# Order of latent norms and modulation pieces, of weight requests, and of the reads of loop bounds, in a two-layer encoder kernel

## The chip, the cores and the metric

One core of a Trainium2 chip runs the kernel. The metric is the device time of one execution in microseconds (us). Engines are named as in the profile: PE is TensorE (PEld its weight loads), DVE is VectorE, ACT is ScalarE, POOL is GpSimd, and SP is SyncE, which here only issues DMAs. A queue name with q (SPq, ACTq) is the side of an engine that issues DMAs.

## The reference

A trunk of two layers over 256 tokens of width 1024, all in float32. Each layer's six modulation vectors, and two more for the key/value side, are `silu(c)` times a 1024-column block of a large matrix:

```
mod = silu(c) @ w_mod[layer] + b_mod[layer]          # 1024 x 6144 per layer; w_mod_kv: 1024 x 2048
# layer 0: h += g1 * retention(modulate(rms_norm(h)));  h += g2 * moe(modulate(rms_norm(h)))
# then once: keys and values
a    = modulate(rms_norm(h)) @ w_kv_a                # 128 latents and 64 rotary columns
c_kv = rms_norm(a[:, :128]); k_rope = rope(a[:, 128:])
k_nope, v = split(c_kv @ w_kv_b)                     # 8 heads
# layer 1: q from rms_norm(xn @ w_q_a) @ w_q_b, softmax attention under a block mask, @ w_o
h += g1 * mix;  h += g2 * moe(modulate(rms_norm(h)))
out = rms_norm(h) * final_norm
```

The mixture of experts takes the best of 4 groups and the best 2 of its 4 experts for each token. 16 experts have three matrices of 2 MB each, `w_gate`, `w_up` and `w_down`, so each layer reads some 100 MB of expert weights.

## The kernel before

**Ring and pieces.** All large weights stream through `ring`, six slots of 2 MB. SP issues the loads in one written order; ahead of each it waits (`released`) until the slot's last user is done. In the stretch that the diff touches the order is `MLA_ITEMS`: the four latent projections (kva, qa, kvb, qb), modulation pieces 20 to 25, the two halves of the output projection (wo0, wo1), pieces 26 and 27. A vector's product with `silu(c)` comes in two pieces; each has four steps on DVE (`mod_main`, a multiply at L1514 or multiply-adds at L1516) that sum into `part`. Vector 10 is pieces 20 and 21, vector 11 is 22 and 23, vector 12 is 24 and 25, vector 13 is 26 and 27. PE then sums the partitions of `part` with a product by ones: `gate_sum` (L604) for gates 10 and 13, whose result DVE adds to `gate` (`gate_store`, L1532), and `row_sum` (L611) for shift and scale, vectors 11 and 12. ACT copies the two row sums out and turns them with two small DMAs (`turned`, L1231); DVE uses them in `vectors` (L1538) and, after `turn_ffn` on PE (L635), prepares the router in `router_prep`.

**Key/value and query side.** PE forms kv latents (L1015), rotary keys (L1021) and query latents (L1029). DVE multiplies the rotary keys by sine and cosine, does all of piece 22, and only then the norms of the latents (L1806 to L1813), for which ACT has meanwhile summed the squares. PE turns the normed latents (L1039, L1044), forms the keys of 8 heads in four banks (L1053), the values (L1060), rotary queries (L1070) and queries (L1082); DVE and ACT copy the banks out, and POOL forms the rotary keys and queries. Before the first scores (L1094) stands row sum 11. After the eight heads PE runs the output projection (L1143) in eight blocks of four matmuls (`wo0`, then `wo1`, for two halves of the tokens and two of the columns); row sum 12, `turn_ffn` and `fixed_logits` (L787) stand between the blocks. A float32 matmul is two records in the trace.

**The experts.** SP loads pair 0's gates and ups (j = 0 to 3) into the ring, each when its slot is released. Pair 0's downs have room outside the ring, `down0` and `down1`; their load waits, in the second layer, for attention's end (`att_o`). Then follow pair 1's gates and the rest. After routing, `rounds(pair, ...)` runs PE's loop over slots of 64 tokens: gather (L865), gates (L890), ups (L903), downs (L921). Its bounds are numbers in memory, which DVE writes at L1714 (`bounds_ready`) and each engine reads into a register (`value_load`). The second layer's counts go on from the first's, so the first bound of `bounds[1]` equals entry `PAIRS` of `bounds[0]`. Each slot of the ring is released by semaphores that PE raises in `rounds`. `keep_warm` is a matmul whose result nobody uses.

Of the kernel before, what the change touches and what calls it, by code (L numbers as in the profile page):

```python
# [19 lines left out]
RH, RDK = 4, 256  # L20
MH, NOPE, ROPE, VH = 8, 128, 64, 128
# [4 lines left out]
PAIRS = NE // 2  # L26
SLOTS = 64
ROUNDS = SEQ // SLOTS
# [61 lines left out]
MOD_STORED = {}  # L90
# [39 lines left out]
def build_kernel(nc, t, out):  # L130
    with ExitStack() as ctx:
# [228 lines left out]
        def _(sp):  # L360
# [79 lines left out]
            for l in range(2):  # L440
                base = MOE_AT[l]

                for j in range(4):
                    released(base - RING + j)
                    load(base + j, matrix(l, 0, j))
                if l == 0:
                    sp.wait_ge(o_done, 2 * RH)
                else:
                    sp.wait_ge(att_o, MH)
                sp.dma_start(down0.rearrange("p (a k) n -> p a k n", a=2), matrix(l, 0, 4)).then_inc(spare_in[0], 16)  # L450
                last = matrix(l, 0, 5)
                sp.dma_start(down1[0], last[:, 0]).then_inc(spare_in[1], 16)
                for j in range(2):
# [86 lines left out]
        def _(pe):  # L540
# [5 lines left out]
            def keep_warm(n, b):  # L546

                for _ in range(n):
                    pe.matmul(bank[b][:], ones, cst[:, 0:512], start=True, stop=True)  # L549
# [241 lines left out]
            def experts(l):  # L791
                n = 1 + 2 * l

                def turn_h(tt, f):

# [50 lines left out]
                pe.matmul(bank[4][:, NE:2 * NE], ones, chosen[:, 0, :], start=False, stop=True).then_inc(ranked, 1)  # L846
                keep_warm(1, 5)
                pe.wait_ge(y_ready, 2 * n + 2)
                pe.wait_ge(bounds_ready, l + 1)
                pe.wait_ge(table_ready, l + 1)  # L850
                if l:
                    pe.wait_ge(mod_stored, MOD_STORED[(13, 1)])
                if l == 0:
                    pe.sem_inc(S["info_done"], 1)

                def rounds(pair, begin, end, here, w, last=False):
# [3 lines left out]
                    with pe.Fori(begin, end) as u:  # L860
# [56 lines left out]
                        def down(n2, f):  # L917
# [7 lines left out]
                            return ins  # L925

                        up(0, range(KT)).then_inc(S["up_done"], 1)
                        up(1, range(KT // 2))
# [56 lines left out]

                rounds(0, bound(slice(0, 1), 0) if l else 0, bound(slice(1, 2), 1), here0, w0)
                rounds(1, bound(slice(1, 2), 1), bound(slice(2, 3), 1),
# [132 lines left out]
            pe.wait_ge(qr_mult, 4)  # L1120
            row_sum(11, mla_bank[6])
            pe.wait_ge(qb_act, 2)
# [15 lines left out]
            for i in range(2):  # L1138
                w = item(f"wo{i}", 0).rearrange("p (k n) -> p k n", k=4)
                for tt in range(TT):  # L1140
                    for n in range(2):
# [6 lines left out]
                        elif tt == 1 and n == 1:  # L1148
                            ins.then_inc(wo_used, 1)
                        if (i, tt, n) == (0, 1, 0):  # L1150
                            row_sum(12, mla_bank[6])
# [250 lines left out]
        def _(dve):  # L1402
# [396 lines left out]
            for i in range(2):  # L1799
                w = trig[:, 1, i:i + 1, :].to_broadcast([P, 2, SEQ])  # L1800
                dve.tensor_tensor(mprod[:, i, :].rearrange("p (f s) -> p f s", f=2),
                                  mla_bank[5][:].rearrange("p (f s) -> p f s", f=2), w, ALU.mult).then_inc(kr_mult, 1)
            mod_main(22)

# [13 lines left out]
            gate_store(10, 1, mla_bank[3])  # L1818
            for b in (2, 4):
                dve.wait_ge(kv_done, b)  # L1820
                dve.tensor_copy(knT[:, 2 * (b - 1):2 * b, :], mla_bank[b][:].rearrange("p (k s) -> p k s", k=2)).then_inc(kv_dve, 1)
            for b in (1, 3):
                dve.wait_ge(kv_done, 4 + b + 1)
                dve.tensor_copy(vm[:, b // 2, 512:1024], mla_bank[(5, 6, 7, 0)[b]][:]).then_inc(kv_dve, 1)
            mod_main(23, (0, 1))

            dve.wait_ge(kr_ready, 5)
            for f in range(2):
                dve.wait_ge(qb_done, 1 + f)
                for i in range(2):  # L1830
                    w = trig[:, 1, i:i + 1, :].to_broadcast([P, 2, SEQ])
                    dve.tensor_tensor(mprod[:, 2 * f + i, :].rearrange("p (f s) -> p f s", f=2),
                                      mla_bank[5 + f][:].rearrange("p (f s) -> p f s", f=2), w, ALU.mult).then_inc(qr_mult, 1)
            mod_main(23, (2, 3))
            for b in (2, 4):
# [27 lines left out]
            for hd in range(MH):  # L1863
                head_scale(hd)
                if hd + 2 < MH:
                    head_max(hd + 2)
            for m in range(24, N_MOD):
                mod_main(m)
# [201 lines left out]
```

## Time and profile before

| | us |
|---|---|
| median of 3 runs (lowest, highest) | 928.96 (927.59, 932.24) |
| the profiled execution | 930.08 |
| its span, first to last instruction | 928.3 |
| PE busy | 859.1 (93%) |
| DVE, ACT, POOL busy | 325.8, 172.5, 162.2 |
| share of the chain that ended last: PE, DMA, DVE, issue | 76%, 16%, 3%, 2% |
| mean granted clock of PE | 0.967 |

The stages of the span, by the timeline: first layer's retention to about 285, its routing to 296, its experts to 537; the key/value and query side from there to 597; attention to 623; output projection to 654; second routing to 669; second experts to 919; final norm to the end. DMA has 317.15 MB to move; in the expert stages it runs at some 420 GB/s over long stretches.

### The profile page before, as it was taken

The page shows a single profiled execution, that of the slowest core. Times are in us where ns is not written, and L with a number is a line of the kernel's source. Part 1 is how long each engine was busy: PE and PEld are TensorE (multiplying, and loading weights), DVE is VectorE, ACT ScalarE, POOL GpSimd, SP SyncE. Part 2 cuts the span into 40 slices and gives each one's busy share as a digit, 9 for nine tenths or more (in the row PEclk, how much of TensorE's full clock was granted, in tenths as well). Part 3 has the DMA queues.
Part 4 walks back from the last instruction along what each step waited for, and adds up shares of the span by engine and source line. Part 5 has one row for each costly group of instructions (what it writes and reads, how often), then busy time and mean ns, then how long its engine had stood idle before and what let it go on. Part 6 is the DMA issues. An engine that isn't in the chain of part 4 may idle for free.

```text
span 928.3 us, 12079 instructions
## 1 busy us (share of the span) xinstructions
PE 859.1 (93%) x4367; PEld 480.4 (52%) x4368; DVE 325.8 (35%) x592; ACT 172.5 (19%) x342; POOL 162.2 (17%) x272
## 2 busy tenths in 40 slices
PE   6999999999998999999888876999699999999985
PEld 4787444444445455544454365774455554555442
DVE  2836676864104111111111185677411111111103
ACT  2100121222003222212011030250322212211111
POOL 0023000000016322221011041301622221111011
PEclk9999999999998999999899877999899999999999
DMA  9999989989383799999999954596799999399995
GB/s 323 387 357 376 373 330 376 348 316 383 146 320 139 307 424 402 420 422 422 423 423 415 331 207 182 187 361 267 309 397 423 416 396 423 141 390 423 423 379 179
DMA packets 69686, 317.15 MB, mean 342 GB/s; under 512 B 9976, under 2 KB 10107, under 8 KB 44303
## 3 DMA queue, kind: packets, MB, share of 16 engines
q1 hardware_dynamic: 61274, 304.42, 82.0%
q0 software_dynamic: 4976, 8.40, 3.6%
q10 hardware_dynamic: 3396, 3.80, 1.3%
q8 instruction: 26, 0.43, 0.2%
q14 instruction: 14, 0.11, 0.0%
HBM read 311.31 MB, written 15.20 MB: 352 GB/s over the span
## 4 chain that ended last, share of the span: by engine, by line
PE 76%; DMA 16%; DVE 3%; issue 2%; ACT 1%; SPq 1%; ACTq 0%; DVEq 0%; POOL 0%; POOLq 0%
PE bank L903 13%; PE bank L722 12%; DMA ring<-in_moe_w_up 11%; PE bank L921 8%; PE bank L890 8%; PE bank L763 6%; PE bank L865 5%; PE bank L663 4%; DMA h<-outs 3%; PE bank L1143 3%; PE bank L715 1%; PE bank L1096 1%; PE bank L913 1%; DMA outs<-arena,row_id 1%; PE bank L549 1%
## 5 line engine op out<-in xcount | busy, mean ns | idle before, releaser
L903 PE MATMUL bank<-ring,arena 128*64 128x256 f32 x1088 | 130.1, 394 | 16.7 <-DMA ring<-in_moe_w_up 16.7
L921 PE MATMUL bank<-ring,arena 128*64 128x512 f32 x480 | 112.2, 609 | 5.8 <-issue 5.8
L1763 DVE TENSOR_TENSOR arena<-bank,arena 128x256 f32<-128x256 f32 x34 | 20.9, 614 | 272.4 <-PE bank L903 272.4
L903 PEld LDWEIGHTS bank<-ring,arena 128*64 128x64 f32 x1088 | 83.2, 142 | 64.2 <-issue 34.1
L1516 DVE SCALAR_TENSOR_TENSOR part<-ring,cpad,part 128x1024 f32<-128x1024 f32 x84 | 111.2, 1324 | 3.2 <-DVE part L1516 0.7
L722 PE MATMUL bank<-ring,xnT 128*128 128x512 f32 x256 | 111.2, 593 | 0.0
L890 PE MATMUL bank<-ring,arena 128*64 128x512 f32 x480 | 106.3, 596 | 0.0
L722 PEld LDWEIGHTS bank<-ring,xnT 128*128 128x128 f32 x256 | 48.5, 190 | 59.3 <-issue 59.2
L865 PEld LDWEIGHTS bank<-arena,y 128*128 128x128 f32 x544 | 66.5, 203 | 19.6 <-issue 19.6
L865 PE MATMUL bank<-arena,y 128*128 128x128 f32 x544 | 69.7, 290 | 5.1 <-issue 5.1
L921 PEld LDWEIGHTS bank<-ring,arena 128*64 128x64 f32 x480 | 34.0, 140 | 64.3 <-issue 62.3
L890 PEld LDWEIGHTS bank<-ring,arena 128*64 128x64 f32 x480 | 33.2, 137 | 60.2 <-issue 59.9
L1313 ACT ACTIVATE arena<-bank,modc,scale 128x128 f32<-128x128 f32 x68 | 25.6, 456 | 186.9 <-PE bank L865 186.9
L1929 POOL DMA_INDIRECT outs<-arena,row_id x17 | 18.0, 1056 | 220.7 <-DVE arena L1773 138.9
L1773 DVE SCALAR_TENSOR_TENSOR arena<-bank,info,gate 128x512 f32<-128x512 f32 x34 | 25.5, 751 | 78.7 <-PE bank L921 78.7
L1905 POOL TENSOR_TENSOR h<-h,acc 128x512 f32<-128x512 f32 x6 | 7.6, 1264 | 242.6 <-DVE acc L1642 242.6
L1924 POOL TENSOR_SCALAR arena<-slot_id,place_two 128x64 f32<-128x64 f32 x108 | 45.8, 445 | 5.5 <-POOL slot_id L1939 3.0
L663 PE MATMUL bank<-xnT,ring 128*128 128x256 f32 x192 | 41.9, 380 | 0.0
L663 PEld LDWEIGHTS bank<-xnT,ring 128*128 128x128 f32 x192 | 36.5, 190 | 5.3 <-DVE xnT L1469 0.4
L1754 DVE TENSOR_SCALAR arena<-bank,scale,modc 128x128 f32<-128x128 f32 x68 | 23.3, 404 | 28.9 <-PE bank L865 28.9
L1143 PE MATMUL bank<-ring,arena 128*128 128x512 f32 x64 | 28.5, 598 | 0.5 <-issue 0.5
L763 PE MATMUL bank<-ring,y 128*128 128x512 f32 x64 | 28.0, 592 | 0.0
(304 smaller groups left out, 871.4 us busy)
## 6 DMA issues: line engine op xcount, KB each, us to landing
ring<-in_moe_w_up SPq DMA_DIRECT2D x64, 1024.0 KB, 12.1
ring<-in_moe_w_gate SPq DMA_DIRECT2D x56, 1024.0 KB, 14.8
ring<-in_moe_w_down SPq DMA_DIRECT2D x56, 1024.0 KB, 15.7
ring<-in_w_mod SPq DMA_DIRECT2D x48, 1024.0 KB, 11.9
ring<-in_ret_w_in SPq DMA_DIRECT2D x24, 1024.0 KB, 7.8
ring<-in_w_mod_kv SPq DMA_DIRECT2D x8, 1024.0 KB, 12.7
ring<-in_ret_w_out SPq DMA_DIRECT2D x8, 1024.0 KB, 12.9
arena<-in_moe_w_down SPq DMA_DIRECT2D x2, 2048.0 KB, 12.1
```

What stands on the lines that cost most here:

```text
L663: ins = pe.matmul(o[:, f * SEQ:(f + 1) * SEQ], w[:, k, c:c + P], xnT[:, k, :], start=(f == 0 and k == 0), stop=(f == 1 and k == KT - 1))
L722: ins = pe.matmul(pair[tt][:], xnT[:, k, tok(tt)], w[:, k, :], start=(k == 0), stop=(k == KT - 1))
L763: ins = pe.matmul(bank[2 * tt + n][:], yT(4 * i + kk)[:, tok(tt)], w[:, kk, n * 512:(n + 1) * 512], start=(i == 0 and kk == 0), stop=(i == ...
L865: ins = pe.matmul(bank[4 + k // 4][:, (k % 4) * P:(k % 4 + 1) * P], y[:, tt, k * P:(k + 1) * P], chosen_slots[:, tt, :], start=(tt == 0), ...
L890: ins = pe.matmul(bank[0][e * 64:(e + 1) * 64, :], xgT[:, k, e * 64:(e + 1) * 64], w(e, k), start=(k == 0), stop=(k == KT - 1))
L903: ins = pe.matmul(bank[1 + f][e * 64:(e + 1) * 64, 0:256], xgT[:, k, e * 64:(e + 1) * 64], w(2 + e, k)[:, f * 256:(f + 1) * 256], start=(k ...
L921: ins = pe.matmul(bank[6 + n2][e * 64:(e + 1) * 64, :], hidT[:, k, e * 64:(e + 1) * 64], w(4 + e, k)[:, n2 * 512:(n2 + 1) * 512], start=(k ...
L1143: ins = pe.matmul(mla_bank[(5, 7, 0, 4)[2 * tt + n]][:], oT[:, 4 * i + kk, tok(tt)], w[:, kk, n * 512:(n + 1) * 512], start=(i == 0 and kk ...
L1313: ins = A(xgT[:, k, :], bank[5][:, tok(j)], ACT.Identity, bias=modc[:, MOD_COL[l] + 24 + k:MOD_COL[l] + 25 + k], scale=scale[:, 1 + 2 * l, ...
L1516: ins = dve.scalar_tensor_tensor(o, w[:, k, :], c, o, ALU.mult, ALU.add)
L1773: dve.scalar_tensor_tensor(yg[:, s], bank[6 + n2][:], info[:, 1:2], gate[:, 2 * l + 1, s], ALU.mult, ALU.mult).then_inc(S["yg_ready"], 1)
L1924: ins = pool.tensor_scalar(dst[:, tt, e * SLOTS:(e + 1) * SLOTS], slots, places[:, tt, e:e + 1], None, ALU.is_equal)
```

## The change

Five edits, in the order of the file:

1. SP: in the second layer the two loads of pair 0's down weights, with their wait for attention's end, go ahead of the four loads of pair 0's gates and ups. In the first layer the order stays.
2. PE, `experts`: the first bound of the second layer is read at the start of the stage, from the first layer's array. The second bound is read right after the wait for `bounds_ready`, ahead of the waits for `y_ready` and `table_ready`. The second layer has one more `keep_warm` matmul.
3. PE: the second layer's wait for gate 13's stores moves from ahead of `rounds` to ahead of the up matmuls in each round.
4. PE: row sum 11 moves from ahead of the first scores to after the output projection's first block; row sum 12 moves one block later.
5. DVE: piece 22 no longer stands ahead of the latent norms. Its first two steps stand ahead of the two key copies, its last two where the first two of piece 23 stood; those move to where the last two of 23 stood, and these to after the last head.

```diff
--- before.py
+++ after.py
@@ -440,16 +440,26 @@
             for l in range(2):
                 base = MOE_AT[l]
 
-                for j in range(4):
+                def ahead(j):
                     released(base - RING + j)
                     load(base + j, matrix(l, 0, j))
+
+                last = matrix(l, 0, 5)
+
+                def outside_down():
+                    if l == 0:
+                        sp.wait_ge(o_done, 2 * RH)
+                    else:
+                        sp.wait_ge(att_o, MH)
+                    sp.dma_start(down0.rearrange("p (a k) n -> p a k n", a=2), matrix(l, 0, 4)).then_inc(spare_in[0], 16)
+                    sp.dma_start(down1[0], last[:, 0]).then_inc(spare_in[1], 16)
+
+                if l:
+                    outside_down()
+                for j in range(4):
+                    ahead(j)
                 if l == 0:
-                    sp.wait_ge(o_done, 2 * RH)
-                else:
-                    sp.wait_ge(att_o, MH)
-                sp.dma_start(down0.rearrange("p (a k) n -> p a k n", a=2), matrix(l, 0, 4)).then_inc(spare_in[0], 16)
-                last = matrix(l, 0, 5)
-                sp.dma_start(down1[0], last[:, 0]).then_inc(spare_in[1], 16)
+                    outside_down()
                 for j in range(2):
                     released(base - 2 + j)
                     load(base + 4 + j, matrix(l, 1, j))
@@ -791,6 +801,8 @@
             def experts(l):
                 n = 1 + 2 * l
 
+                begin0 = pe.value_load(bounds[0][0:1, PAIRS:PAIRS + 1], min_val=PAIRS, max_val=ROUNDS * PAIRS) if l else 0
+
                 def turn_h(tt, f):
 
                     for j in range(4):
@@ -844,12 +856,11 @@
                 ins.then_inc(counted, 1)
                 pe.matmul(bank[4][:, 0:TT * NE], tri, chosen[:].rearrange("p t e -> p (t e)"), start=True, stop=False)
                 pe.matmul(bank[4][:, NE:2 * NE], ones, chosen[:, 0, :], start=False, stop=True).then_inc(ranked, 1)
-                keep_warm(1, 5)
+                keep_warm(1 + l, 5)
+                pe.wait_ge(bounds_ready, l + 1)
+                second = pe.value_load(bounds[l][0:1, 1:2], min_val=1, max_val=ROUNDS * PAIRS * (l + 1))
                 pe.wait_ge(y_ready, 2 * n + 2)
-                pe.wait_ge(bounds_ready, l + 1)
                 pe.wait_ge(table_ready, l + 1)
-                if l:
-                    pe.wait_ge(mod_stored, MOD_STORED[(13, 1)])
                 if l == 0:
                     pe.sem_inc(S["info_done"], 1)
 
@@ -924,6 +935,8 @@
                                                     start=(k == 0), stop=(k == 3))
                             return ins
 
+                        if l:
+                            pe.wait_ge(mod_stored, MOD_STORED[(13, 1)])
                         up(0, range(KT)).then_inc(S["up_done"], 1)
                         up(1, range(KT // 2))
                         turn_hidden(0)
@@ -983,7 +996,7 @@
                 def bound(at, least):
                     return pe.value_load(bounds[l][0:1, at], min_val=least, max_val=ROUNDS * PAIRS * (l + 1))
 
-                rounds(0, bound(slice(0, 1), 0) if l else 0, bound(slice(1, 2), 1), here0, w0)
+                rounds(0, begin0, second, here0, w0)
                 rounds(1, bound(slice(1, 2), 1), bound(slice(2, 3), 1),
                        lambda j, f: arrived(base + 4 + j, halves=(f,)), lambda j, k: in_ring(base + 4 + j, j, k))
                 rounds(2, bound(slice(2, 3), 1), bound(slice(3, 4), 1), here2, w2)
@@ -1118,7 +1131,6 @@
                 pe.matmul(b[:, P:SEQ], v[:, 1, :], probT[:, hd % 2, SEQ:SEQ + P], start=False, stop=True).then_inc(att_o, 1)
 
             pe.wait_ge(qr_mult, 4)
-            row_sum(11, mla_bank[6])
             pe.wait_ge(qb_act, 2)
             pe.wait_ge(qb_dve, 2)
             pe.wait_ge(qr_ready, 2)
@@ -1147,7 +1159,9 @@
                             ins.then_inc(mix_done, 1)
                         elif tt == 1 and n == 1:
                             ins.then_inc(wo_used, 1)
-                        if (i, tt, n) == (0, 1, 0):
+                        if (i, tt, n) == (0, 0, 0):
+                            row_sum(11, mla_bank[6])
+                        if (i, tt, n) == (0, 1, 1):
                             row_sum(12, mla_bank[6])
                         if (i, tt, n) == (1, 0, 0):
                             turn_ffn(3, mla_bank[2])
@@ -1800,7 +1814,6 @@
                 w = trig[:, 1, i:i + 1, :].to_broadcast([P, 2, SEQ])
                 dve.tensor_tensor(mprod[:, i, :].rearrange("p (f s) -> p f s", f=2),
                                   mla_bank[5][:].rearrange("p (f s) -> p f s", f=2), w, ALU.mult).then_inc(kr_mult, 1)
-            mod_main(22)
 
             dve.wait_ge(lat_sq, 4)
             dve.tensor_scalar(var[:, 0:2], msq[:, 0:2], 1.0 / KVL, EPS, ALU.mult, ALU.add).then_inc(lat_ms, 1)
@@ -1817,12 +1830,13 @@
             gate_store(10, 0, mla_bank[5])
             gate_store(10, 1, mla_bank[3])
             for b in (2, 4):
+                mod_main(22, (b // 2 - 1,))
                 dve.wait_ge(kv_done, b)
                 dve.tensor_copy(knT[:, 2 * (b - 1):2 * b, :], mla_bank[b][:].rearrange("p (k s) -> p k s", k=2)).then_inc(kv_dve, 1)
             for b in (1, 3):
                 dve.wait_ge(kv_done, 4 + b + 1)
                 dve.tensor_copy(vm[:, b // 2, 512:1024], mla_bank[(5, 6, 7, 0)[b]][:]).then_inc(kv_dve, 1)
-            mod_main(23, (0, 1))
+            mod_main(22, (2, 3))
 
             dve.wait_ge(kr_ready, 5)
             for f in range(2):
@@ -1831,7 +1845,7 @@
                     w = trig[:, 1, i:i + 1, :].to_broadcast([P, 2, SEQ])
                     dve.tensor_tensor(mprod[:, 2 * f + i, :].rearrange("p (f s) -> p f s", f=2),
                                       mla_bank[5 + f][:].rearrange("p (f s) -> p f s", f=2), w, ALU.mult).then_inc(qr_mult, 1)
-            mod_main(23, (2, 3))
+            mod_main(23, (0, 1))
             for b in (2, 4):
                 dve.wait_ge(qb_done, 2 + b)
                 dve.tensor_copy(qnT[:, 2 * (b - 1):2 * b, :], mla_bank[b][:].rearrange("p (k s) -> p k s", k=2)).then_inc(qb_dve, 1)
@@ -1864,6 +1878,7 @@
                 head_scale(hd)
                 if hd + 2 < MH:
                     head_max(hd + 2)
+            mod_main(23, (2, 3))
             for m in range(24, N_MOD):
                 mod_main(m)
             vectors(3, cols[:, :, 10:12])
```

## Rows read from the trace of the kernel before

**Rows 1.** The timeline, key/value part; start us, us, engine, line, operation [idle before]
```profile
550.95 7.07 PE L1021 MATMUL bank<-arena,ring 128*128 128x256 f32 x32
...
565.60 0.20 ACT L1351 ACTIVATION_READ_ACCUMULATOR xnT<-bank 128x1 f32 x1
...
567.31 0.75 DVE L1514 TENSOR_SCALAR part<-ring,cpad 128x1024 f32<-128x1024 f32 x1 [7.71 <-issue]
...
568.09 3.92 DVE L1516 SCALAR_TENSOR_TENSOR part<-ring,cpad,part 128x1024 f32<-128x1024 f32 x3
...
572.18 0.17 DVE L1806 TENSOR_SCALAR stat<-stat 128x2 f32<-128x2 f32 x1 [0.16 <-DVE part L1516]
...
573.57 0.69 PE L1039 MATMUL bank<-cst,arena 128*128 128x128 f32 x2 [6.92 <-DVE arena L1811]
...
575.26 5.87 PE L1053 MATMUL bank<-arena,ring 128*128 128x256 f32 x16
...
576.29 1.28 DVE L1532 TENSOR_TENSOR gate<-bank,gate 128x512 f32<-128x512 f32 x2
...
585.55 3.71 PE L1070 MATMUL bank<-arena,ring 128*128 128x256 f32 x16 [0.99 <-DVE arena L1824]
```

**Rows 2.** Busy time by stretch; clock, DMA share and GB/s at the end
```profile
core 0: us, PE busy (x) PEld busy (x) DVE busy (x) ACT busy (x) POOL busy (x), PEclk, DMA share, GB/s
576.00:580.00 4.00, 4.00 (x11) 3.12 (x11) 2.27 (x4) 0.60 (x1) 3.84 (x5) 0.52 0.01 2
...
648.00:652.00 4.00, 4.00 (x12) 1.87 (x11) 0.69 (x1) 2.63 (x4) 1.78 (x2) 1.00 0.00 0
...
668.00:672.00 4.00, 2.54 (x12) 2.57 (x13) 0.00 (x0) 0.00 (x0) 2.07 (x2) 0.50 1.01 420
...
740.00:744.00 4.00, 4.00 (x32) 1.90 (x28) 0.61 (x1) 1.67 (x2) 0.00 (x0) 1.00 0.86 332
```

**Rows 3.** The timeline, end of the second routing
```profile
663.51 1.10 PE L549 MATMUL bank<-cst 128*128 128x512 f32 x2
...
664.31 0.16 DVE L1714 CAST bounds<-boundf 1x16 int32<-1x16 f32 x1
...
666.40 1.29 DVE L1532 TENSOR_TENSOR gate<-bank,gate 128x512 f32<-128x512 f32 x2 [0.21 <-issue]
...
669.47 6.64 PE L865 MATMUL bank<-arena,y 128*128 128x128 f32 x32 [4.85 <-issue]
```

**Rows 4.** The timeline, then the chain of waits, first routing
```profile
294.45 0.16 DVE L1714 CAST bounds<-boundf 1x16 int32<-1x16 f32 x1
...
296.48 5.45 PE bank L865 x32
```

**Rows 5.** Waits, from 540 us: total us, times, longest
```profile
PE bank L903 <- DMA ring<-in_moe_w_up: 5.7, 2, 4.6
```

**Rows 6.** The timeline, VectorE and GpSimd side by side
```profile
547.89 5.04 DVE L1516 SCALAR_TENSOR_TENSOR part<-ring,cpad,part 128x1024 f32<-128x1024 f32 x3
...
548.71 3.15 POOL L2032 COPY ring<-ring 128x512 f32<-128x512 f32 x2
```

**Rows 7.** The timeline, from the first scores to the output projection's end
```profile
596.12 1.05 PE L611 MATMUL bank<-part,cst 128*32 128x512 f32 x4
...
620.42 0.75 DVE L1514 TENSOR_SCALAR part<-ring,cpad 128x1024 f32<-128x1024 f32 x1
...
623.14 10.54 PE L1143 MATMUL bank<-ring,arena 128*128 128x512 f32 x24 [0.52 <-issue]
...
640.63 0.18 DVE L1538 TENSOR_TENSOR modc<-turned,cols 128x16 f32<-128x16 f32 x1
...
650.50 0.29 PE L787 MATMUL bank<-shifted,cst 128*128 128x16 f32 x2
```

**Rows 8.** The timeline, the small DMAs of the first layer
```profile
250.26 1.18 ACTq L1231 DMA_DIRECT2D turned<-arena  x2
...
256.71 0.19 DVE L1538 TENSOR_TENSOR modc<-turned,cols 128x16 f32<-128x16 f32 x1 [21.91 <-DMA turned<-arena]
```

**Rows 9.** DMA issues, from 540 us: KB each, median us to landing
```profile
acc<-in_moe_w_down SPq DMA_DIRECT2D x1, 1024.0 KB, 24.9
```

## Prediction

> **What bounds the kernel now.** I read the page's chain of work first: TensorE carries three quarters of it, and most of the remainder is waiting for expert weights. So a microsecond counts only where TensorE stands still, or where TensorE sets when a ring slot comes free. Then I read the order of instructions in the stretches that the diff touches.
>
> *Latents* [rows 1]. ScalarE ends the last sum of squares at 565.60 + 0.20 = 565.80. VectorE starts the norm step (L1806) only at 572.18: it has first taken up modulation piece 22, waited for its weights until 567.31, and spent 0.75 + 3.92 us on it. TensorE sits idle 6.92 us ahead of its latent transposes (L1039). It then runs the key matmuls (L1053) at the low clock: 16 records take 5.87 us, where 32 of the same tile size took 7.07 us at full clock (L1021). The clock row for 576 to 580 shows 0.52, nearly all of it the lower level, 1.2 of 2.4 GHz [rows 2].
>
> *Second routing* [rows 3]. The bounds are written at 664.31 + 0.16 = 664.47, and the first gather (L865) starts at 669.47, 5.0 us later. TensorE waits for VectorE's two gate adds (L1532, to 667.69) and reads two bounds after that. The gather then takes 6.64 us at clock 0.50 [rows 2]. In the first routing no gate add stands between: bounds at 294.61, gather at 296.48 (1.87 us later), 5.45 us long [rows 4].
>
> *Expert stage.* In the second one TensorE waits for up weights 5.7 us over two places [rows 5]. But the DMA queue is empty at 648 to 652, and has gaps again at 740 to 744 [rows 2]: there the stream has caught up with the slots that TensorE releases, so what follows is timed from TensorE.
>
> **The change part by part.** All terms are against the profiled execution (span 928.3, time 930.08), which lies 1.1 above the median of the runs.
>
> A. *Norms ahead of piece 22.* The norm step can start 0.17 us after the squares (it started about that long after VectorE's own last step): 565.97 instead of 572.18, **6.2 us**. TensorE's transposes come to 567.4. It is free by then: its idle time before L1039 began at 573.57 - 6.92 = 566.65. Bounds: 5.5 if handing over from ScalarE costs more, 6.4 if it costs nothing.
>
> B. *Clock of the key matmuls.* With 0.7 us of idle time in place of 6.92 I expect the clock to stay up. L1053 would take 7.07 / 2 = 3.5 instead of 5.9: 2.3 us less. Its third bank also waits for the gate add of vector 10 (L1532). That add shifts to about 570.1 to 571.4, where the first two banks end at 570.8, so 0.6 comes back. Gain **1.8** with the transposes' own; bounds 0 (clock falls anyway) and 2.6.
>
> C. *What takes piece 22's place.* Its first two quarters now stand ahead of the two key copies, its last two where 23's first half was, that half where 23's second was, and 23's second half behind the last head. The first quarter costs 0.75, the second 3.92 / 3 = 1.3. In the new frame VectorE does 571.4 to 572.2, copy, 572.9 to 574.2, copy; the value matmuls end at about 576.5, so both quarters and the value copies fit beside them. The query matmuls (L1070, 585.55 before) start near 577.5, 8.0 earlier (A + B). Cost taken: 0; bounds 0 and 0.7. One row speaks against it: a multiply-add piece took 5.04 us for three beside GpSimd's copies, against 3.92 without [rows 6], 0.37 more each, and GpSimd now forms the rotary keys beside these two quarters. That is 0.7 us, inside the cover that I count.
> The Trainium skill (SBUF — State Buffer, Who interferes with whom) says that a VectorE instruction with two SBUF inputs contends with a GpSimd one that reads SBUF, and that the loser blocks for the whole instruction. The trace agrees with the slowing; a block through several rotary steps would be worse than the 0.7 used here, and no row shows one.
>
> D. *Row sum 11* leaves the place before the first scores, where it ran 596.12 to 597.17 beside the last query copy, and joins the output projection, where TensorE has no gap: 24 records run on from 623.14 [rows 7]. Gain ahead 0 (at most 0.2), cost behind **1.0**. Row sum 12 comes one block (3.5 us) later. The first projection block ends at about 618.6 in the new frame, and VectorE has finished piece 23 by 620.42 - 8.0 + 2.6 (two steps of 1.3) = 615.0, so neither sum waits.
>
> E. *VectorE after attention* has 2.6 us more. Piece 27 ended by 640.63 and now ends near 635.2. The vectors then need row sum 12 (done 631.2) and the two small DMAs that follow it. In the first layer these went out at 250.26 and were used at 256.71, 6.45 us later [rows 8]; so 632.0 + 6.45 = 638.5, and router preparation, some 2 us, ends near 640.6. TensorE asks for it (L787, 650.50 before) at 643.5. Cost 0, cover 2.9 us; if the DMAs need more, the excess is lost.
> The Trainium skill (DMA: Bandwidth & Descriptors, Queues, rings and completion order) says that a DMA engine takes the queue rows in turn, packet by packet. By that rule the small DMAs don't wait behind SyncE's megabytes, and the first layer's 6.45 us agree.
>
> F. *SyncE.* Three megabytes of the first pair's down weights now go out when attention ends, into time in which the queue was later empty. Ahead of it SyncE waits for piece 23, since piece 27 reuses its slot: piece 27 is requested near 615.1 instead of ahead of attention's end, and is needed at 630. Gates 0 and 1 come after pieces 24 and 25. Some 9.4 MB at about 420 GB/s are in by 637.7, up 0 by 642.7, before the projection ends (647). So the expert stage starts with 7.4 us less DMA work behind it, while TensorE comes closer by G and H, 4.3 us. The stream still catches up before the fourth pair's gates, so the two stalls of 5.7 us stay, timed from TensorE. Cost and gain 0. Bounds: minus 1.2 (the small stall goes) and plus 4.3 (a rival).
>
> G. *Bounds ahead of the last waits.* The start of the second expert stage (the end of the first) is read long before, beside matmuls already queued. The wait for the gate store moves to the first up matmuls, some 10 us after the gather starts. One more warming matmul (1.10 us) ends at 665.6 in the old frame, and the read of the bound runs beside it. I take the first routing's 1.87 us from bounds to gather: gain 5.0 - 1.9 = **3.1**. Bounds: 2.1, if the read starts only when the warming is over (665.6, and the 1.77 us from 667.70 to 669.47 as its price), and 3.6. The wait stands in every round: cheap and beside queued matmuls, 0. The first routing's own gain: 0, bounds 0 and 0.3, since its warming matmuls already cover the read.
>
> H. *Clock of the first gather.* With a shorter idle stretch and one more matmul it is the likeliest to look like the first layer's: 6.64 - 5.45 = **1.2**. Bounds 0 and 3.3 (all of it at full clock).
>
> Sum: 6.2 + 1.8 - 1.0 + 3.1 + 1.2 = 11.3. Profiled 918.8; from the median 928.96 it gives **917.7 us**.
>
> **The rivals.**
> - *Both clocks stay low.* For: the first routing had fallen to half although idle for little, and the four transposes are thin work. Against: the clock is full at 648 to 652 and through the projection. Then A - D + G = 8.3: 920.7.
> - *Both clocks stay full.* B and H at their ends: 11.3 + 0.5 + 2.1 = 13.9: 915.0.
> - *The expert stage is paced by transfers.* What TensorE wins after attention's end (G + H, 4.3) returns as longer waits for up weights. For: 5.7 us of such waits now. Against: the gaps at 740 to 744, and F. 922.0.
> - *The norms were not what held the latents* (the change doesn't do there what it says: the next stage waits for something as late, such as GpSimd's keys). Then only G + H - D = 3.3: 925.7. Against: the idle times in [rows 1] name VectorE alone.
> - *Slower: piece 27 lands late.* It is the one large load pushed from before attention's end to after it, with 3 MB of down weights and the gates crowding in. The longest landing of this stage is 24.9 us [rows 9]. VectorE could start piece 27 as late as 636.5 without making L787 wait (643.5, less 2.0 for the vectors, less 5.2 for four steps), which is 21 us after the request. At 24.9 the loss is 3.5; the gain is used up from 21 + 11.3 = 33 us; at 40 us the kernel stands at 936. The bytes queued bound it at about 643, 28 us, so this is remote.
>
> **How the numbers follow.** Forecast 0.55; clocks low 0.15; clocks full 0.10; paced by transfers 0.12; norms not the cause 0.05; slower 0.03. The forecast's own range is 916 to 920. 8 in 10 takes in the full clocks below and the two partial cases above with a microsecond of scatter: 913.8 to 923.3. What a measurement can tell here is about 0.5%, 4.6 us: faster means under 924.3. All cases but the last two lie there: faster 0.92, same 0.05, slower 0.03.
>
> **What would show it.** A: L1806 within 0.3 us of ScalarE's last square, TensorE's idle time before L1039 under 1 us. B: L1053 in about 4 us, clock 1.0. C: L1070 starting 7.5 to 8.5 earlier. D: L1143 ends 7 earlier, not 8. E: no idle time ahead of L787. F: the empty stretch before the projection's end shorter, piece 27's step on VectorE without a wait, the two waits of the expert stage as long as now. G: 1.9 us from the bounds to the first gather; H: that gather at 5 to 6 us. It is wrong if the gather starts less than 8 us earlier than 669.47, or if the waits for up weights grow by more than 2 us.

## The result and the profile after

The changed kernel takes 922.89 us (median of 20 runs, 920.37 to 929.68), the kernel before 928.78 on the same chip (20 runs). The ratio is 0.9947, with a 95% interval of 0.9932 to 0.9963. It is faster, by 5.9 us; the forecast was 11.3. The range held the time at its upper edge. The profiled execution took 925.25 with a span of 923.5, so the two traces differ by 4.8.

The timeline of the changed kernel from the latents to the first gather (columns as in [rows 1]; line numbers are 10 to 15 higher than before, DVE L1552 for instance is L1538 of before, and shift again by a few in each experiment's kernel):

```profile
567.15 0.20 ACT L1365 ACTIVATION_READ_ACCUMULATOR xnT<-bank 128x1 f32 x1
567.39 0.17 DVE L1819 TENSOR_SCALAR stat<-stat 128x2 f32<-128x2 f32 x1 [6.19 <-ACT xnT L1365]
568.77 0.44 PE L1052 MATMUL bank<-cst,arena 128*128 128x128 f32 x2 [0.58 <-DVE arena L1824]
570.05 1.89 PE L1066 MATMUL bank<-arena,ring 128*128 128x256 f32 x8
...
572.24 1.26 DVE L1528 TENSOR_SCALAR part<-ring,cpad 128x1024 f32<-128x1024 f32 x1
572.38 1.99 PE L1066 MATMUL bank<-arena,ring 128*128 128x256 f32 x8 [0.44 <-DVE gate L1546]
574.14 1.81 DVE L1530 SCALAR_TENSOR_TENSOR part<-ring,cpad,part 128x1024 f32<-128x1024 f32 x1
...
578.78 3.70 PE L1083 MATMUL bank<-arena,ring 128*128 128x256 f32 x16 [0.98 <-DVE arena L1838]
...
616.36 3.67 PE L1155 MATMUL bank<-ring,arena 128*128 128x512 f32 x8 [0.52 <-issue]
...
617.20 1.63 SPq L454 DMA_DIRECT2D arena<-in_moe_w_down  x1
618.88 0.47 SPq L455 DMA_DIRECT2D arena<-in_moe_w_down  x1
...
633.16 1.58 ACTq L1245 DMA_DIRECT2D turned<-row_late  x2
...
646.76 0.18 DVE L1552 TENSOR_TENSOR modc<-turned,cols 128x16 f32<-128x16 f32 x1 [10.33 <-DMA turned<-row_late]
...
648.81 0.40 PE L797 MATMUL bank<-shifted,cst 128*128 128x16 f32 x2 [3.75 <-DVE shifted L1569]
649.06 5.38 PE L1155 MATMUL bank<-ring,arena 128*128 128x512 f32 x8
...
657.05 0.63 PE L813 MATMUL bank<-cst,h 128*128 128x128 f32 x4 [0.68 <-DVE h L1667]
...
665.83 0.16 DVE L1728 CAST bounds<-boundf 1x16 int32<-1x16 f32 x1
667.13 3.81 PE L876 MATMUL bank<-arena,y 128*128 128x128 f32 x32
```

Read against [rows 1], [rows 3] and [rows 7]: the norms, the bounds and the gather are as wanted or better. But VectorE now stands 10.33 us for the two small `turned` DMAs (the turned halves of the last vector), and TensorE 3.75 us behind it. The chain of waits of the changed kernel (start, us, what) passes through that transfer:

```profile
631.51 1.01 PE bank L621 x4
...
633.16 1.03 ACTq L1245
634.23 12.51 DMA turned<-row_late
...
648.76 0.61 DVE acc L1656
649.43 2.50 POOL h L1920 x2
651.95 1.15 ACT y L1304 x2
```

Busy time by stretch, columns as in [rows 2]:

```profile
638.00:642.00 4.00, 4.00 (x10) 1.85 (x11) 0.00 (x0) 0.00 (x0) 0.00 (x0) 1.00 1.02 424
...
644.00:646.00 2.00, 1.06 (x3) 0.19 (x1) 0.00 (x0) 0.00 (x0) 0.00 (x0) 1.00 0.70 276
646.00:648.00 2.00, 0.00 (x0) 0.00 (x0) 1.10 (x5) 0.00 (x0) 0.00 (x0) 1.00 0.03 5
648.00:652.00 4.00, 3.19 (x6) 1.49 (x7) 2.48 (x6) 0.05 (x1) 2.57 (x3) 0.70 0.00 0
668.00:672.00 4.00, 4.00 (x35) 3.54 (x35) 2.27 (x6) 1.73 (x4) 2.19 (x5) 1.00 1.01 422
```

The DMA share is full until 645.2 and falls to nothing by 646.7: SyncE's megabytes had all landed, and VectorE went on with the small DMAs' data at 646.76. Below, the backlog is what SyncE has requested and has not yet moved, and its end is the moment at which the DMA share has fallen to about half, here 645.4. The waits, answering to [rows 5] (total us, times, longest):

```profile
PE bank L914 <- DMA ring<-in_moe_w_up: 5.2, 2, 4.5
```

Where the 4.8 us came from, by TensorE's marks in both traces:

| stretch | before | after | gain | forecast |
|---|---|---|---|---|
| start to the last transposes before the key/value part (no edit in it) | 540.61 | 542.18 | -1.57 | 0 |
| to the output projection (A, B, C) | 82.53 | 74.18 | 8.35 | 8.0 |
| projection to its last turns, L801, now L813 (D, E) | 32.80 | 40.69 | -7.89 | -1.0 |
| to the gather (G) | 13.53 | 10.08 | 3.45 | 3.1 |
| the gather, to the first gate matmul (H) | 6.97 | 4.16 | 2.81 | 1.2 |
| the rest (F) | 251.86 | 252.21 | -0.35 | 0 |

### The profile page after: what moved, and what is told of

It reads as the page before. It is cut to its first block, busy times and chain, and to the rows that moved or that the text cites. A ratio compares the mean times of both kernels' runs of the same rounds, so it can differ in the third digit from the quotient of the medians.

```text
span 923.5 us, 12083 instructions
## 1 busy us (share of the span) xinstructions
PE 857.3 (93%) x4369; PEld 476.6 (52%) x4370; DVE 326.9 (35%) x592; ACT 172.5 (19%) x342; POOL 164.4 (18%) x272
## 4 chain that ended last, share of the span: by engine, by line
PE 74%; DMA 18%; DVE 3%; issue 2%; ACT 2%; SPq 1%; ACTq 0%; POOL 0%; DVEq 0%; POOLq 0%
PE bank L914 12%; PE bank L732 12%; DMA ring<-in_moe_w_up 8%; PE bank L932 8%; PE bank L901 8%; PE bank L773 6%; DMA h<-outs 6%; PE bank L876 5%; PE bank L673 4%; DMA outs<-arena,row_id 2%; PE bank L1155 2%; PE bank L725 1%; DMA turned<-row_late 1%; PE bank L559 1%; PE bank L1109 1%
## 5 line engine op out<-in xcount | busy, mean ns | idle before, releaser
L876 PEld LDWEIGHTS bank<-arena,y 128*128 128x128 f32 x544 | 64.0, 197 | 14.6 <-issue 14.6
L876 PE MATMUL bank<-arena,y 128*128 128x128 f32 x544 | 67.2, 283 | 0.1
L1920 POOL TENSOR_TENSOR h<-h,acc 128x512 f32<-128x512 f32 x6 | 7.5, 1264 | 249.4 <-DVE acc L1656 249.4
L1155 PE MATMUL bank<-ring,arena 128*128 128x512 f32 x64 | 30.4, 629 | 0.5 <-issue 0.5
```

The costliest lines, as they stand in the source:

```text
L876: ins = pe.matmul(bank[4 + k // 4][:, (k % 4) * P:(k % 4 + 1) * P], y[:, tt, k * P:(k + 1) * P], chosen_slots[:, tt, :], start=(tt == 0), ...
L1155: ins = pe.matmul(mla_bank[(5, 7, 0, 4)[2 * tt + n]][:], oT[:, 4 * i + kk, tok(tt)], w[:, kk, n * 512:(n + 1) * 512], start=(i == 0 and kk ...
```

## The experiments

Theory: three megabytes of down weights ahead of the gates lengthen SyncE's backlog, and the small DMAs that ScalarE issues land only when it is empty. Rival one: VectorE's later row sum 12 (edit D) makes `turned` late. Rival two: what G and H win is taken back by the expert stage. In the tables and texts, "after start" counts from the first matmul of the output projection.

**e1: the order of SyncE's loads as before.**

```
-                if l:
-                    outside_down()
                 for j in range(4):
                     ahead(j)
-                if l == 0:
-                    outside_down()
+                outside_down()
```

> The changed kernel with SyncE's order of before: pair 0's down weights behind its gates and ups. Theory (backlog): the two small DMAs that turn row sums 11 and 12 took 13.6 us from issue to use because some 10 MB, the 3 MB of down weights among them, had been requested ahead of them; without the downs they are used within about 6 us of their issue, VectorE's wait of 10.3 us shrinks to under 4, TensorE no longer waits ahead of the fixed logits (3.75 us now), its clock stays full, and the kernel takes 6 to 7 us less than the changed one, about 916. Rival (the downs' lead is needed): the expert stage loses up to 7.4 us (3 MB at 420 GB/s), so 920 to 924. Rival (late row sum): the wait stays at 8 us or more, 922 to 923.

Measured: 920.3 us (6 runs), ratio 0.9928 (0.9904 to 0.9953). Its timeline, then its waits for up weights:

```profile
631.74 1.58 ACTq L1242 DMA_DIRECT2D turned<-row_late  x2
...
639.17 0.19 DVE L1549 TENSOR_TENSOR modc<-turned,cols 128x16 f32<-128x16 f32 x1 [4.17 <-DMA turned<-row_late]
...
643.47 0.29 PE L794 MATMUL bank<-shifted,cst 128*128 128x16 f32 x2
```
```profile
PE bank L911 <- DMA ring<-in_moe_w_up: 7.8, 2, 4.5
```

From issue to use 7.4 us instead of 13.6, and TensorE's wait is gone. The same row sums stand in it, so rival one can't be the cause. But the waits for up weights grow from 5.2 to 7.8. In e4 below, where TensorE is as far along as in e1 (34.67 and 34.55 us from the projection's start to its last turns) and the downs are early, they are 5.2 again. So the early downs do help the expert stage, by 2.6 us in this pair of traces (the kernels that have the bounds' edit and all downs early show 4.9 to 6.2), which I had put at nothing.

**e2: the downs after the small DMAs have landed, ahead of the ups.**

```
                 for j in range(4):
+                    if l and j == 2:
+                        sp.wait_ge(vecs_in, 128)
+                        outside_down()
                     ahead(j)
```

> The changed kernel, but pair 0's downs (and then its ups) are requested only once the small DMAs have landed, behind the two gates. Backlog theory: small DMAs used 4 to 7 us after issue, no wait of TensorE at the fixed logits, 915.5 to 917, and the 3 MB still move ahead of the projection's end. If the downs' lead is worth something this one is faster than the kernel with the downs last, otherwise equal. Late row sum theory: 922 to 923, as the changed kernel.

Measured: 916.16 us (6 runs), ratio 0.989 (0.9864 to 0.9916), an interval apart from the changed kernel's. Its timeline, and its busy time by stretch:

```profile
629.41 1.58 ACTq L1246 DMA_DIRECT2D turned<-row_late  x2
...
632.47 0.38 SPq L454 DMA_DIRECT2D arena<-in_moe_w_down  x1
632.61 0.18 DVE L1553 TENSOR_TENSOR modc<-turned,cols 128x16 f32<-128x16 f32 x1
```
```profile
626.00:628.00 2.00, 2.00 (x7) 0.60 (x7) 1.77 (x2) 0.00 (x0) 0.00 (x0) 1.00 0.98 414
630.00:632.00 2.00, 2.00 (x6) 0.76 (x4) 1.93 (x3) 0.00 (x0) 0.00 (x0) 1.00 0.19 61
```

The small DMAs go out as the backlog ends, are in 3.1 us later (SyncE passes its wait at 632.47), and VectorE takes them up at 632.61, straight after piece 27. This gives both: no stall at the projection, and 5.4 us of waits for ups, about the changed kernel's.

**e3: row sum 12 one block earlier, as before the change** (`(i, tt, n) == (0, 1, 0)`).

> The changed kernel with row sum 12 one block (3.5 us) earlier, where it stood before; the small DMAs are issued 3.5 us earlier, behind the same megabytes. Backlog theory: they are used at the same moment as in the changed kernel, near 646 in its frame, when the queue has drained, so VectorE's wait grows and the time stays within 1 us of the changed kernel (922 to 923.5). Late row sum theory (fixed latency): they are used 3.5 us earlier and the kernel takes about 3.5 us less, 919.4.

Measured: 924.65 us (9 runs), ratio 0.9947 (0.9924 to 0.997).

```profile
631.31 1.58 ACTq L1245 DMA_DIRECT2D turned<-row_late  x2
...
648.10 0.18 DVE L1552 TENSOR_TENSOR modc<-turned,cols 128x16 f32<-128x16 f32 x1 [10.08 <-DMA turned<-row_late]
```

Issued 3.4 us earlier after start (13.37 against 16.80), used at the same time after start (30.16 against 30.40). The latency stretched from 13.6 to 16.8 us. So it is not a duration of the DMA but a wait for a point in time, the end of the backlog. Rival one is out.

**e4: the same turning by GpSimd's queue** (four DMAs of 64 partitions with a semaphore of their own, in place of ScalarE's two).

```
+                    pool.dma_start(turned[64 * a:64 * a + 64, 3, r, :],
+                                   row_late[...]).then_inc(vecs_late, 16)
```

> The changed kernel, but GpSimd issues the turning of row sums 11 and 12 (four small software DMAs) in place of ScalarE. If the backlog holds every queue's transfers, the vectors come near 646 again or later and the time stays at 922 to 925. If each queue gets its turn and only ScalarE's queue is held up by SyncE's, they land some 4 to 6 us after issue, near 638, and the time is 916 to 917.

Measured: 918.07 us (6 runs), ratio 0.9897 (0.9877 to 0.9918). Timeline and stretches:

```profile
630.77 2.19 POOL L2069 DMA_DIRECT2D turned<-row_late  x4 [44.64 <-ACT row_late L1241]
...
637.99 0.19 DVE L1555 TENSOR_TENSOR modc<-turned,cols 128x16 f32<-128x16 f32 x1 [4.22 <-DMA turned<-row_late]
```
```profile
636.00:638.00 2.00, 2.00 (x6) 0.82 (x5) 0.01 (x1) 0.00 (x0) 0.00 (x0) 1.00 1.03 411
640.00:642.00 2.00, 2.00 (x6) 0.95 (x5) 1.19 (x2) 0.00 (x0) 1.32 (x2) 1.00 1.01 422
```

The engines were saturated until about 643, with the early downs in front as in the changed kernel, and yet `turned` was there at 637.99, 7.2 us after the issue. The same bytes through another queue are not held. So full DMA engines as such are not the cause; what holds them is tied to ScalarE's queue under SyncE's backlog. The edit also makes four DMAs of 2 KB out of two of 4 KB, and no run keeps that apart from the change of queue.

The DMA packets in the traces show how they are held. A packet is one piece of a transfer on one of the 16 DMA engines; the counts are those of each queue.

| stretch | SyncE's packets | the small DMAs' packets |
|---|---|---|
| changed kernel, 633 (issue) to 637 | 226 | 0 |
| 637 to 645 | 454 | 55 |
| 645 to 647 | 36 | 205 |
| e4, 630.5 (issue) to 634 | 196 | 0 |
| 634 to 638 | 223 | 128 |

In both kernels the first small packet moves some 4 us after the issue. From then on ScalarE's queue does move, but with one packet for eight of SyncE's, 6 to 8 in a microsecond; the same rate stands in e3 (635 to 647) and e9 (634 to 637). So some 200 of its 260 packets are left at the backlog's end and then go within two microseconds. GpSimd's queue moves one packet for one of SyncE's at the best (101 against 111 in 635 to 637), and it has 128 in all.

**e9 and e11: two sizes between.** e9 puts 1 MB of the downs ahead (`down1`) and 2 MB (`down0`) behind the ups. e11 keeps all the downs ahead and makes the ups wait (`vecs_in`, 128).

> The changed kernel with only 1 MB of the downs ahead of the gates and ups, the other 2 MB behind them. Backlog theory (the small DMAs are used when the queue of megabytes has drained): 2 MB less is 5 us less, so the vectors come about 25 us after the output projection's start in place of 30.4, TensorE no longer waits ahead of the fixed logits, 917 to 919. Rival (a saturated DMA holds small transfers for some 13 us whatever is queued): 30 us after the start, 922 to 923.

> The changed kernel with the downs first, but the two ups requested only once the small DMAs have landed. Backlog theory: the 2 MB of up 0, requested at the same time as the small DMAs, no longer count; vectors about 25 us after the projection's start, 917 to 919. If only what was requested well before the small DMAs holds them, no change: 30 us, 922 to 923.

Measured: e9 919.8 us (4 runs), 0.9898 (0.9863 to 0.9932); e11 919.24 (4 runs), 0.9901 (0.9867 to 0.9935). Their small DMAs took 8.4 and 8.5 us, and were used 1.1 and 1.2 us after the backlog's end (near 637.6 and 636.7). Each has 2 MB less in front than the changed kernel, which is 5.0 us at 420 GB/s, and they are used 5.2 and 5.1 us earlier after start. All kernels with the new latent order and both row sums in the projection, in us after start (e8 is told below):

| kernel | issued | used | projection start to last turns |
|---|---|---|---|
| e2 | 16.80 | 20.00 | 33.97 |
| e8 | 16.80 | 20.97 | 33.97 |
| e1 | 16.81 | 24.24 | 34.55 |
| e4 | 17.07 | 24.29 | 34.67 |
| e7 | 16.80 | 24.36 | 34.65 |
| e9 | 16.80 | 25.22 | 35.51 |
| e11 | 16.80 | 25.32 | 35.61 |
| e3 | 13.37 | 30.16 | 40.44 |
| changed kernel | 16.80 | 30.40 | 40.69 |

In e2 and e8 the small DMAs find the backlog gone and take 3.2 and 4.2 us. The constants are read off this table: all nine lie on 33.97 + (used - 23.66), where that is positive, within 0.1 us. So the delay of `turned` passes one to one into the time from 23.66 on, and the changed kernel lost 6.7 us by it. It also shows how thin the cover is. In e9 and e11 the fixed logits (L797 of the changed kernel) have no wait; TensorE waits at the turns behind them. The chain after shows why: behind `turned` VectorE also holds the first gated sums of the projection (L1656), behind them stand GpSimd's additions (L1920) and ScalarE's square sum (L1304), and these come late first.

**e5, e6 and e7: the parts alone, each on the kernel before.** e5 has the early downs only; e6 the read-ahead of the bounds with the second warming matmul and the moved wait; e7 the latent norms, the pieces and the row sums.

> The kernel before with the first of the five edits alone: pair 0's downs requested when attention ends. Backlog theory: the queue then drains near 646 in the frame of before, the small DMAs issued at 635.3 are used near 646 in place of 640.6; router preparation ends near 648, ahead of the fixed logits at 650.5, so TensorE hardly waits (0 to 1 us) and the 3 MB of lead buy nothing or the small stall at 788: 927 to 929.5 (before: 928). If the early downs were a gain of their own: 924 or less.

> The kernel before with the bounds read ahead, one more warming matmul and the gate wait moved, nothing else. In the changed kernel the stretch from the last h transposes to the gather's end shrank from 20.5 to 14.2 us. If that is this edit's alone: 6.3 us less, 921.7. If the experts then come closer to their transfers (stalls for up weights 7.8 us instead of 5.2 where the downs go out late): 922 to 925, with the waits for up weights at 8 us or more. Forecast's terms G + H: 923.7.

> The kernel before with the order of norms, pieces and row sums of the changed one, SyncE's order and the bounds as before. Backlog theory: output projection starts 8 us earlier than before; small DMAs used 7 to 8 us after issue; TensorE waits at most 0.5 us at the fixed logits; gain 8.3 - 1.0 - 0.6 = 6.7, 921.3. If the late row sum were the cause of the wait of 10.3 us: 925 or more.

| | us (runs) | ratio (95%) |
|---|---|---|
| e5 | 930.13 (12) | 1.0027 (1.0007 to 1.0047) |
| e6 | 929.82 (12) | 1.0005 (0.9987 to 1.0023) |
| e7 | 922.4 (9) | 0.9935 (0.9908 to 0.9961) |

e5 is slightly slower: issued at 632.33 and used at 645.46, the small DMAs are held there too, and a wait of 2.11 us stands before its turns. So e5 doesn't show what early downs are worth without that wait. In e6 the gather comes 3.9 us earlier and is 2.8 shorter. Timeline and waits of e6:

```profile
664.28 0.16 DVE L1717 CAST bounds<-boundf 1x16 int32<-1x16 f32 x1
665.55 3.81 PE L866 MATMUL bank<-arena,y 128*128 128x128 f32 x32
...
785.87 8.03 PE L904 MATMUL bank<-ring,arena 128*64 128x256 f32 x48 [4.54 <-DMA ring<-in_moe_w_up]
...
803.46 2.72 PE L866 MATMUL bank<-arena,y 128*128 128x128 f32 x22
```
```profile
PE bank L904 <- DMA ring<-in_moe_w_up: 9.2, 3, 4.5
```

A later round's gather starts at 803.46, against 803.35 before. All 6.7 us are given back by then: 5.0 us of waits for ups lie before it against 1.2 in the kernel before, and the 48 matmuls behind the long wait take 8.03 us instead of 5.40 (granted clock 0.85 in 780 to 803, where before had 1.00). Rival two is true for e6, because the weights there arrive no earlier than before. With the downs ahead (e2) the waits stay at 5.4. e7 is worth 6.0 us by itself. With its order in place the bounds alone add little (e1, ratio 0.9928 against e7's 0.9935), and bounds and early downs together add 4 us (e2, 0.989; its interval just touches e7's, that of e10 below is clear of it). So the edit to the bounds needs the early downs. Whether the early downs need it in turn isn't shown: no run has e7 with the downs behind the small DMAs and nothing else.

**e8: e2 with one warming matmul instead of two** (`keep_warm(1, 5)`).

> The kernel of e2 (downs behind the small DMAs) with one warming matmul in the second routing, as before the change, in place of two. Theory (the second matmul keeps the clock up): the gather runs at the low clock, 5.4 to 6.6 us in place of 3.8, 1.6 to 2.8 us longer: 917.8 to 919. Rival (the shorter idle stretch does it): the gather stays at 3.8 and starts up to 1 us earlier if the matmul, not the read, ends last: 915.2 to 916.2.

Measured: 918.34 us (6 runs), ratio 0.9889 (0.986 to 0.9918), in time not to be told from e2's. e8, then e2:

```profile
658.74 0.16 DVE L1729 CAST bounds<-boundf 1x16 int32<-1x16 f32 x1
660.00 5.39 PE L877 MATMUL bank<-arena,y 128*128 128x128 f32 x32 [0.96 <-DVE arena L1739]
```
```profile
654.95 0.16 DVE L1729 CAST bounds<-boundf 1x16 int32<-1x16 f32 x1
656.22 3.81 PE L877 MATMUL bank<-arena,y 128*128 128x128 f32 x32
```

The second warming matmul delays nothing (1.10 and 1.11 us from the bounds to the gather). Without it TensorE idles 0.96 us, and the gather takes 1.6 us more, at a granted clock of 0.50 from 660 to 663, the lower level.

But two warming matmuls don't always keep the clock up. Of the nine kernels that have them, five run the gather in 3.81 us (changed kernel, e2, e3, e6, e10). In the other four (e1, e4, e9, e11) the clock falls during the warming itself, and the gather takes 4.05 to 4.44 us without idle time ahead of it. In e1 the granted clock is 0.65 in 658 to 659 and 0.50 in 659 to 661:

```profile
657.48 2.98 PE L556 MATMUL bank<-cst 128*128 128x512 f32 x4
660.25 4.44 PE L873 MATMUL bank<-arena,y 128*128 128x128 f32 x32
```

There the gather starts 1.8 to 2.2 us after the bounds, as the warming matmuls end, and not 1.1: at the lower level the second one is in the way. What decides between the two groups is not shown.

**e10: e2 with row sum 12 one block earlier.**

> The kernel of e2 with row sum 12 one block earlier, as before the change. There the small DMAs find a nearly empty queue; issued 3.5 us earlier they are behind the gates instead. Backlog theory: used no earlier than some 2 us before those of e2, so the same time within 1 us (915.5 to 917); downs and ups are requested up to 2 us earlier, which buys nothing.

Measured: 915.96 us (6 runs), ratio 0.9861 (0.9836 to 0.9886): the best of all, though not to be told from e2's 916.16. `turned` is issued 3.4 us earlier than in e2 (13.36 after start) and used 19.99 after start, when VectorE has ended piece 27; they had landed 5.0 us after their issue, for SyncE passes its wait at 629.75. The stretch from projection to turns is 33.97 again. With the cover whole, the place of the row sum makes no difference. Both e2 and e10 beat the kernel before and the changed one.

## Why the prediction was wrong, point by point

**The failed step is E**: "the two small DMAs ... were used at 256.71, 6.45 us later [rows 8]; so 632.0 + 6.45 = 638.5 ... Cost 0, cover 2.9 us; if the DMAs need more, the excess is lost." The issue was placed rightly (16.9 us after start, measured 16.80), the rest was not. The latency was taken as a constant of the DMA; it measured 3.2 to 16.8 us, for the same bytes, by SyncE's backlog (e2, e3). And F, which moves 3 MB ahead of these DMAs, was costed on the expert stage alone, though E's own DMAs had to go out behind it. F even gave the drain, "up 0 by 642.7"; that number belonged in E. The cover was wrong too: counted to the fixed logits it was 2.9, but it ends at 23.66 after start, and the forecast use (638.5, from a start at 615.1) lies 23.4 after start. That left 0.3. Cost 6.7 instead of 0. The rule of the Trainium skill that I set beside it (DMA: Bandwidth & Descriptors, Queues, rings and completion order), queue rows served in turn packet by packet, does not describe what ScalarE's queue did here: one packet for eight of SyncE's, 13.6 us, and landing only with the backlog's end. GpSimd's queue in e4 is near it, with 101 packets against 111.

The row that gave the 6.45 us could have warned. In the kernel before, SyncE had requested 2 MB of ups (`in_moe_w_up`) from 248.72 on, ahead of the small DMAs of 250.26:

```profile
248.72 8.11 SPq L398 DMA_DIRECT2D ring<-in_moe_w_up  x4
...
DMA  0000000000096789999999995210949989989899
```

The second line is the DMA share in tenths, in 40 slices of 0.425 us from 245 on. It is full to about 255.2 and down to a tenth near 256, and VectorE took the data at 256.71, after waiting for it. So the 6.45 us were themselves a wait for the end of a short backlog, and did not bear out the rule. Nor was the second layer of the kernel before like it:

```profile
635.33 1.58 ACTq L1231 DMA_DIRECT2D turned<-row_late  x2
```

These were used at 640.63 [rows 7], 5.3 us later, when VectorE had ended piece 27; SyncE's load had run out near 637.4.

A. *Right.* The norm step starts 0.04 us after the square sum's end (567.35), idle time before the transposes 0.58.

B. *Right.* The key matmuls take 3.88 us with 0.44 between them, at clock 1.0; the second half waits for the gate add, as said.

C. *Right.* The query matmuls start 6.77 earlier, with the drift of 1.57 ahead of them that is 8.34 (said: 7.5 to 8.5). The quarters slow beside GpSimd to 1.26 and 1.81 us instead of 0.75 and 1.3, inside the cover. GpSimd's additions for the rotary keys slow as well, from 0.71 us to 1.16 and 1.70.

D. *Right.* Kernels with both sums in the projection take 33.97 where before took 32.80: 1.17, said 1.0. Row sum 12's later place costs nothing (e3, e10).

F. *Nearly right in sum, not in reason.* The waits for ups are 5.2. But they would be 7.8 without the early downs (e1); the edit pays for the earlier TensorE and is not idle cover.

G. *Right, a little too small.* Bounds to gather 1.14 us instead of 5.0, 3.9 less; the read hides whole beside the warming matmuls. Routing ahead of it took 0.4 more (8.78 against 8.37), which leaves the 3.45 of the table.

H. *Undersized.* I took the first layer's half-clock gather [rows 4]. The gather runs at full clock in the changed kernel, 3.81 us, where [rows 3] had 6.64: 2.8 against 1.2. Four of the experiments' kernels, with up to 4.44 us, show that this was partly luck. The end that I gave as 3.3 was nearer.

The sum again: 11.3, less 6.7 (E), less 1.6 of drift in a stretch without an edit, plus 1.6 (H), with 0.2 from the rest: 4.8. With E mended alone (e2) the kernel stands at 916.16, 1.5 below the forecast. The rival with both clocks full adds 0.5 for B where B's own bound gives 0.8: 914.8 in place of 915.0, which changes nothing. Of the rivals none was this one. "Piece 27 lands late" looked at the right queue and the wrong transfer: piece 27's last step ends near 636.4 on VectorE without a wait worth naming.

What stays open: why ScalarE's queue gets one packet in beside eight of SyncE's and GpSimd's one beside one. The traces show the rates, not the mechanism, nor whether the smaller DMAs of e4 have a part in it. By the rate of some 7 packets in a microsecond the 260 would land after 41 us (an estimate, with the 4 us ahead of the first) even if the backlog went on; no run has one that long. The drift of 1.57 us ahead of the key/value part lies within the scatter of the profiled runs (the same transposes begin between 538.3 in e7 and 545.3 in e3) and is not explained either. Nor is a step of 1.6 us in the stretch behind it, up to the projection: 74.2 to 74.3 us in the changed kernel, e1 and e7, and 72.6 in the seven others with the new order; 80.3, 80.6 and 82.5 in e5, e6 and the kernel before. By the mean start of the projection, 622.1 with the old order and 614.2 with the new, A to C gained 7.9.

## What to carry to other kernels

When megabytes are queued earlier, list every small DMA that is issued while they drain, on all queues, and cost each by the end of the backlog, not by its latency elsewhere. Place bulk requests behind a wait for the small ones (e2: 6.7 us in the stretch that waited, for one wait), or send the small ones by a queue that isn't held (e4). And follow the waiting instruction's whole engine: the cover ends at the first thing queued behind it, which needn't be the consumer that one has in mind. Where a stage is paced by transfers, moving compute forward pays only if the transfers move forward too (e6 against e2).

## What the runs showed of the hardware

- Two DMAs of 4 KB each, from ScalarE's queue, took 3.2 and 4.2 us from issue to use with SyncE's backlog gone (e2, e8), and 7.4 (e1), 8.4 (e9), 13.6 (changed kernel) and 16.8 us (e3) with more and more of it outstanding; in these the use followed the backlog's end by 0.4 to 1.4 us. By GpSimd's queue, as four of 2 KB, the same bytes took 7.2 us under a full load (e4).
- Beside SyncE's backlog ScalarE's queue moved 55 packets while SyncE's moved 454 (changed kernel), GpSimd's 101 while SyncE's moved 111 (e4).
- Two of VectorE's steps on a piece took 1.26 and 1.81 us beside GpSimd, where they take 0.75 and 1.3 otherwise, and GpSimd's instructions of 32x256 beside them up to 1.70 instead of 0.71 (changed kernel).
- The gather, 32 matmuls, took 6.64 us after 4.85 us of idle time (kernel before), 5.39 after 0.96 (e8), and with none 3.81 (e2 and four others) or 4.05 to 4.44 (e1, e4, e9, e11), where the clock fell to its lower level in the matmuls ahead of it.
